# Attention scores as three products of rounded parts instead of one fp32 product, in a three-layer fp32 kernel

## What is computed

```python
# layer 1, heads of 64 channels, 8 + 8 heads, blocks of 128 queries
s = einsum('bqhd,bkhd->bhqk', qb, k) * scale + cq[..., None] - cum[..., None, :]   # forgetting heads
s = einsum('bcqhd,bckhd->bhcqk', qc, kb) * scale + bias                            # biased heads
# layer 2: 8 stick-breaking heads, 8 latent heads
z = einsum('bqhd,bkhd->bhqk', qb, k) * scale
a = exp(log_sigmoid(z) + suffix)          # suffix: reversed exclusive sum of log_sigmoid(-z)
s = (einsum(q_nope, k_nope) + einsum(q_rope, k_rope)) * scale                      # latent heads
# second block: 4 differential pairs (rotated q, k), 8 heads with three branches each
s = einsum('bqhcd,bkhcd->bhcqk', qb, k) * scale
sc, ss, sw = compressed keys, selected keys, window keys, each einsum(qb, keys) * scale
```

## Time and profile before

| | |
|---|---|
| median of three runs | 2082.27 us |
| the profiled execution | 2084.69 us |
| its span, first to last instruction | 2082.9 us |
| TensorE busy | 2029.1 us (97%), 9900 matmul records |
| VectorE busy | 993.9 us (48%), 1563 instructions |
| ScalarE busy | 904.2 us (43%) |
| GpSimd busy | 865.3 us (42%) |
| mean granted clock of TensorE | 0.995 |

### The profile page before, as it was taken

The page is one execution under the profiler, slowest core; times in us unless marked ns, Lnnn a source line. Parts: engine busy times, 40 slices in busy tenths (PEclk is TensorE's granted clock), DMA queues, the critical chain, the costliest instruction groups (busy, mean ns, idle before and its releaser), DMA issues.

```text
span 2082.9 us, 28463 instructions
## 1 busy us (share of the span) xinstructions
PE 2029.1 (97%) x9900; PEld 1596.8 (77%) x9900; DVE 993.9 (48%) x1563; ACT 904.2 (43%) x1760; POOL 865.3 (42%) x648
## 2 busy tenths in 40 slices
PE   9999999999999999999999999998989999999997
PEld 6777688888887766688888887776667878888886
DVE  6444555322264678652312265666555563223133
ACT  5444543323343664552323356765553343223234
POOL 3222345444454322244444454542114554545454
PEclk9999999999999999999999999999999999999999
DMA  4222122322222111022223232321102322232323
GB/s 157 65 70 84 58 100 93 101 92 101 91 100 91 64 58 42 31 92 100 96 97 100 91 101 71 112 92 41 42 31 71 101 91 97 95 101 92 101 94 109
DMA packets 50580, 177.87 MB, mean 85 GB/s; under 512 B 5536, under 2 KB 5800, under 8 KB 50480
## 3 DMA queue, kind: packets, MB, share of 16 engines
q1 hardware_dynamic: 48096, 172.07, 24.7%
q10 hardware_dynamic: 2384, 4.43, 0.6%
HBM read 174.36 MB, written 2.12 MB: 85 GB/s over the span
## 4 chain that ended last, share of the span: by engine, by line
issue 46%; PE 31%; POOL 19%; DVE 2%; POOLq 1%; ACT 1%; DVEq 0%; ACTq 0%
POOL w_lo L517 19%; PE gemm_banks L542 9%; PE gemm_banks L544 9%; PE gemm_banks L543 9%; PE score_banks L989 1%; PE out_bank L1035 1%; PE score_banks L998 1%; DVE turned L2217 1%; POOLq L511 0%; ACT tmp L1471 0%; POOLq L516 0%; DVE score_banks L1794 0%; DVE x L2313 0%; PE out_bank L1026 0%; PE gemm_banks L961 0%
## 5 line engine op out<-in xcount | busy, mean ns | idle before, releaser
L517 POOL TENSOR_TENSOR w_lo<-raw,w_hi 128x512 fp32r<-128x512 f32 x644 | 865.1, 1365 | 1200.4 <-ACT w_hi L1106 1200.2
L1106 ACT ACTIVATE w_hi<-raw 128x512 fp32r<-128x512 f32 x644 | 370.8, 623 | 782.5 <-PE gemm_banks L544 777.9
L542 PE MATMUL gemm_banks<-h_hi,w_hi 128*128 128x512 f32 x1512 | 612.8, 405 | 4.6 <-POOL w_lo L517 3.0
L544 PE MATMUL gemm_banks<-h_hi,w_lo 128*128 128x512 f32 x1512 | 590.5, 391 | 0.0
L543 PE MATMUL gemm_banks<-h_lo,w_hi 128*128 128x512 f32 x1512 | 589.8, 390 | 0.0
L542 PEld LDWEIGHTS gemm_banks<-h_hi,w_hi 128*128 128x128 f32 x1512 | 282.8, 187 | 98.2 <-issue 35.4
L542 PE MATMUL gemm_banks<-u_hi,w_hi 128*128 128x512 f32 x864 | 339.3, 393 | 5.6 <-POOL w_lo L517 1.5
L543 PE MATMUL gemm_banks<-u_lo,w_hi 128*128 128x512 f32 x864 | 336.3, 389 | 0.0
L544 PE MATMUL gemm_banks<-u_hi,w_lo 128*128 128x512 f32 x864 | 336.3, 389 | 0.0
L544 PEld LDWEIGHTS gemm_banks<-h_hi,w_lo 128*128 128x128 f32 x1512 | 282.8, 187 | 62.5
L543 PEld LDWEIGHTS gemm_banks<-h_lo,w_hi 128*128 128x128 f32 x1512 | 283.4, 187 | 55.7 <-issue 2.9
(11 more groups left out here) (317 smaller groups left out, 1869.0 us busy)
## 6 DMA issues: line engine op xcount, KB each, us to landing
raw<-slabs SPq DMA_DIRECT2D x322, 512.0 KB, 3.3
table<-rel_rows ACTq DMA_DIRECT2D x4, 512.0 KB, 3.5
x<-x_t SPq DMA_DIRECT2D x4, 256.0 KB, 7.0
x<-x_t ACTq DMA_DIRECT2D x4, 256.0 KB, 7.2
cos<-pos SPq DMA_DIRECT2D x2, 256.0 KB, 10.1
y_t<-x SPq DMA_DIRECT2D x2, 256.0 KB, 2.8
y_t<-x ACTq DMA_DIRECT2D x2, 256.0 KB, 2.7
y_t<-x SPq DMA_DIRECT2D x1, 512.0 KB, 2.8
```

The costliest lines, as they stand in the source:

```text
L517: pool.tensor_tensor(w_lo[:, j, part], raw[:, j, part], w_hi[:, j, part].bitcast(F32), ALU.subtract).then_inc(slab_split, 1)
L542: pe.matmul(out, high, rhs_hi, start=first, stop=False)
L544: return pe.matmul(out, low, rhs_hi, start=False, stop=last)
L1106: act.activation(w_hi[:, m % 2, part], raw[:, m % 2, part], ACT.Copy).then_inc(slab_hi, 1)
```

## The change

Each q and k that feeds a score is split by VectorE into a part rounded to fp32r and the rest (also fp32r), right behind its eviction or its rotation. A score is then three fp32r products: high times high, high times low, low times high, for both heads in turn. The columns are widened to at least 256, and so are those of the forget bias L652. The score waits for the parts (`q_parts`, `k_parts`), or for `rope_ready`, which now comes with the second part. The compressed scores take two fp32 products, with the high and with the low part of the query as they are in memory. Latent heads and all else stay. The parts lie in memory that was free or that the full tile leaves (the low part overwrites it); k_win's high part lies in `KT_hi`, k_sel's in the place of `cos1`.

```diff
                 if i == 0:
-                    pe.wait_ge(gemm_free, done["k", p])
+                    pe.wait_ge(q_parts, p + 1)
+                    pe.wait_ge(k_parts, p + 1)
...
+                n = max(w, 2 * P)
                 if p < 4:
...
-                        pe.matmul(SC[:, 2 * b + head, 0:w], fox_of[rows, p, :], fox[rows, 0:w],
+                        pe.matmul(SC[:, 2 * b + head, 0:n], fox_of[rows, p, :], fox[rows, 0:n],
                                   start=True, stop=False, skip_group_check=True)
-                for head in range(2):
-                    rows = slice(HEAD * head, HEAD * (head + 1))
-                    pe.matmul(SC[:, 2 * b + head, 0:w], q_t[rows, p % 2, i * P:w], k_t[rows, p % 2, 0:w],
-                              start=(p >= 4), stop=True, skip_group_check=True).then_inc(scored, 1)
+
+                for queries, keys in ((q_hi, k_hi), (q_hi, k_lo), (q_lo, k_hi)):
+                    for head in range(2):
+                        rows = slice(HEAD * head, HEAD * (head + 1))
+                        last = pe.matmul(SC[:, 2 * b + head, 0:n], queries[rows, p % 2, i * P:w],
+                                         keys[rows, p % 2, 0:n], start=(p >= 4 and queries is q_hi and keys is k_hi),
+                                         stop=queries is q_lo, skip_group_check=True)
+                        if queries is q_lo:
+                            last.then_inc(scored, 1)
...
-                        last = pe.matmul(bank[:, i * CQ:(i + 1) * CQ], QT[:, p % 2, i * P:(i + 1) * P], kcmp[:, :],
-                                         start=True, stop=True)
+                        pe.matmul(bank[:, i * CQ:(i + 1) * CQ], QT_hi[:, p % 2, i * P:(i + 1) * P].bitcast(F32),
+                                  kcmp[:, :], start=True, stop=False)
+                        last = pe.matmul(bank[:, i * CQ:(i + 1) * CQ], QT_lo[:, p % 2, i * P:(i + 1) * P].bitcast(F32),
+                                         kcmp[:, :], start=False, stop=True)
...
                     last.then_inc(gemm_free, 1)
                     dve.wait_ge(gemm_free, c.gemm.at())
+                    if name in "qk":
+                        qk_parts(name, p)
+
+            def qk_parts(name, p):
+
+                full = (q_t, k_t)["qk".index(name)][:, p % 2, :]
+                high = (q_hi, k_hi)["qk".index(name)][:, p % 2, :]
+                link(dve.tensor_copy(high, full))
+                dve.tensor_tensor((q_lo, k_lo)["qk".index(name)][:, p % 2, :], full, high.bitcast(F32),
+                                  ALU.subtract).then_inc((q_parts, k_parts)["qk".index(name)], 1)
...
-                    dve.tensor_tensor(dst, dst, tmp[:, 2 + n % 2, :], ALU.add).then_inc(rope_ready, 1)
+                    added = dve.tensor_tensor(dst, dst, tmp[:, 2 + n % 2, :], ALU.add)
+                    if name == "kc":
+                        added.then_inc(rope_ready, 1)
+                    else:
+                        high, low = parts_of(name, p)
+                        link(added)
+                        link(dve.tensor_copy(high, dst))
+                        dve.tensor_tensor(low, dst, high.bitcast(F32), ALU.subtract).then_inc(rope_ready, 1)
```

More of the change, by code:

```diff
@@ L366, in build @@
         w_hi, w_lo = sb("w_hi", [2, SLAB], F32R), sb("w_lo", [2, SLAB], F32R)
-        cos1, sin1, cos2, sin2 = (sb(n, [S]) for n in ("cos1", "sin1", "cos2", "sin2"))
+        region = ExitStack()
+        cos1 = sb("cos1", [S], F32, region)
+        region.close()
+        region = ExitStack()
+        k_sel_hi = sb("k_sel_hi", [S], F32R, region)
+        region.close()
+        hold = stack.enter_context(nc.sbuf_tensor("region_cos", [P, S], F32))
+        del hold
+        sin1, cos2, sin2 = (sb(n, [S]) for n in ("sin1", "cos2", "sin2"))
         consts, params = sb("consts", [N_CONST]), sb("params", [N_PARAM])
@@ L404, in build @@
         region = ExitStack()
-        k_sel, k_win = sb("k_sel", [S], F32, region), sb("k_win", [S], F32, region)
+        left = ExitStack()
+        k_sel, k_win = sb("k_sel", [S], F32, left), sb("k_win", [S], F32, left)
+        left.close()
+        k_sel_lo, k_win_lo = sb("k_sel_lo", [S], F32R, region), sb("k_win_lo", [S], F32R, region)
         V_sel, V_win = sb("V_sel", [NB, P], F32, region), sb("V_win", [NB, P], F32, region)
@@ L831, in cd_scores @@
                 if i == 0:
[L832 to L836, removed]
+                    pe.wait_ge(q_parts, 8 + p + 1)
+                    pe.wait_ge(k_parts, 8 + p + 1)
+                n = max(w, 2 * P)
+                for queries, keys in ((q_hi, k_hi), (q_hi, k_lo), (q_lo, k_hi)):
+                    for head in range(2):
+                        rows = slice(HEAD * head, HEAD * (head + 1))
+                        last = pe.matmul(SC[:, 2 * b + head, 0:n], queries[rows, p % 2, i * P:w],
+                                         keys[rows, p % 2, 0:n], start=False, stop=queries is q_lo,
+                                         skip_group_check=True)
+                        if queries is q_lo:
+                            last.then_inc(scored, 1)
             def cd_flip(s):
@@ L980, in e_scores @@
                 if br == 0:
-                    keys, need = KTT[:, p % 2, :], max(E_ROPE["q", p], E_ROPE["k", p])
+                    keys, need = (KT_hi[:, p % 2, :], KT_lo[:, p % 2, :]), max(E_ROPE["q", p], E_ROPE["k", p])
                 else:
-                    keys = (k_sel, k_win)[br - 1][:, :]
+                    keys = ((k_sel_hi[:, :], k_sel_lo[:, :]), (KT_hi[:, 0, :], k_win_lo[:, :]))[br - 1]
                     need = max(E_ROPE["nq", p], E_ROPE[("ks", "kw")[br - 1], 0])
@@ L986, in e_scores @@
                     pe.wait_ge(rope_ready, need)
-                for head in range(2):
-                    rows = slice(HEAD * head, HEAD * (head + 1))
-                    pe.matmul(SC[:, 2 * (s % 2) + head, 0:w], QT[rows, p % 2, i * P:w], keys[rows, 0:w], start=True,
-                              stop=True, skip_group_check=True).then_inc(scored, 1)
+                n = max(w, 2 * P)
+                for queries, part in ((QT_hi, 0), (QT_hi, 1), (QT_lo, 0)):
+                    for head in range(2):
+                        rows = slice(HEAD * head, HEAD * (head + 1))
+                        last = pe.matmul(SC[:, 2 * (s % 2) + head, 0:n], queries[rows, p % 2, i * P:w],
+                                         keys[part][rows, 0:n], start=(queries is QT_hi and part == 0),
+                                         stop=queries is QT_lo, skip_group_check=True)
+                        if queries is QT_lo:
+                            last.then_inc(scored, 1)
             def e_flip(s):
```

15 lines of the change are left out of this document (added).

## The result

The changed kernel takes **2133.71 us** (median of 4 runs, 2128.72 to 2136.54) against 2083.37 us before (4 runs, 2082.26 to 2084.53): a ratio of 1.0238, 95% interval 1.0226 to 1.0251. It is slower by 50.3 us, where 25.8 us (2108 us, a range up to 2117) were forecast: the sign was right, the size half of what came. The profiled execution took 2133.45 us, its span 2131.7, 48.8 more than that of before.

What follows compares the result with a forecast made beforehand. TensorE, busy for 97% of the span, was taken as the bound. Its own work -3.8, new waits +23.6 and clock +6 made +25.8 us on 2084.7, 2110.5; less 2.4 for the median, 2108 us, range 2087 to 2117 (forecast's own 2100 to 2117).

Steps and rivals of the forecast that it cites:

- Score passes: TensorE's scores: three rounded passes replace fp32 products in 24 groups of four steps, -0.30 us each, -7.2 us in all.
- A split of 3.2 us: VectorE's CAST and subtraction per tile: 3.2 us if begun behind a started GpSimd instruction, 1.2 us if not.
- no lock: Rival, chance 0.18: the CAST runs during GpSimd's first half, only the subtraction waits; split 2.0 us, kernel 2099 us.
- no collision: Rival, chance 0.12: VectorE gets ahead of GpSimd, which waits instead; every split 1.2 us, kernel 2090 us.
- six passes: Rival, chance 0.03: rounded heads don't run side by side, so six passes per step; +40 in place of -7, 2155 us.
- both other starts: First scores of stick-breaking wait for split k_t, +2.5 us; second block's start waits behind QT's and KT's splits, +3.6 us.
- stick-breaking q: Splits of q for stick-breaking pairs 1 to 3 stand uncovered ahead of the take: 3 x 3.2 = +9.6 us.
- nq: Selected and window part: three nq tile splits end ahead of shares or takes TensorE waits for, 3 x 1.2 = +3.6 us.
- absorbed waits: Rival, chance 0.10: new waits take the place of old TensorE idle time, only -3.8 us is left; 2078.5 us.
- Rest of the first mixer: Steady steps behind the first mixer's start: k's split is covered; 0.3 us added for pair 1.
- Differential part: Second block: splits of k 1 and k 2 have one to two us of cover; +1.6 us for both, bounds 0 and 4.
- Clock: TensorE gaps over 2 us may bring 3.4 us at half speed; four of seven at 1.5 us, +6, bounds 0 and 12.

Runs made afterwards that it cites:

- products_only: Changed kernel without the splits: each tile is rounded once by the instruction that writes it, and all three products read it; 2079.87 us.
- stick_later: Changed kernel with the q splits of stick-breaking pairs 1 to 3 moved from ahead of the take to behind the same step's scans; 2119.73 us.
- diff_whole: Changed kernel with pairs 1 to 3 of the differential part not split and scored by one fp32 product; 2120.30 us.
- diff_shares: Changed kernel with the differential part's splits behind the next step's maxima, take and shares, the shares moved ahead of the next rotation; 2120.10 us.
- combo: Changed kernel with q's splits behind scans, second block's behind maxima, no widening, and shares ahead of rotations in the selected and window part; 2104.23 us.
- diff_later: Changed kernel with only the differential part's splits moved, behind the next step's maxima; the second block's start left as it was; 2128.67 us.
- e_later: Changed kernel with second-block splits moved: at its start behind the next turn's eviction, in the differential part behind the next step's maxima; 2120.36 us.

## Why the prediction was right or wrong

- **Score passes, -7.2, and TensorE's own work, -3.8: right.** The step of 512 takes 0.79 for 0.81, products_only measures -3.5, the compressed scores cost 3.6 for 3.2.
- **A split of 3.2 us behind a started GpSimd, 1.2 otherwise: right.** 3.1 in the stick-breaking step, 3.2 in the differential one, 1.1 where GpSimd rested. The rivals "no lock" and "no collision" are out, and so is that of six passes.
- **First mixer's start, both other starts, stick-breaking q, nq: right.** 2.2 for 2.4; 3.0 for 2.5; 3.2 for 3.6; 8.8 for 9.6; 3.7 for 3.6. stick_later shows the mechanism: 14.0 us less with nothing changed but the place. The rival of absorbed waits is out too.
- **Rest of the first mixer, 0.3: too small.** The prediction said that above 1 us more TensorE waits for each k. In the steady pairs it doesn't, but for the last k it does (its split takes 3.2 us, from 213.01 to 216.25). There TensorE waited for the take already before the change (0.35 us at 214.16), and now it is idle for 2.47 us before the values at 218.43. I had read the steady step and not the last.
- **Differential part, 1.6 with bounds 0 and 4: wrong, 10.0.** This is the step of the waits that failed. It asked what cover the take has and left out who else is behind the split. The maxima are, and through them ScalarE's exponentials, w_hi and w_lo (5.2 of the 10.0 us); evictions (3.0) are too, and only 1.9 is the take's. What is queued behind the split was followed on VectorE and not on to ScalarE's queue and GpSimd's. diff_whole puts all ten at the splits, and diff_shares takes back 8.7 of them.
- **Clock, 4 of 7 gaps at 1.5: the size was right, the count wrong.** A single stretch cost 1.2 to 1.8 us. But six of the seven gaps of the count brought one (that at 702.33 didn't), two of them a double one, for 11.6 us in place of 6; the last k of the first mixer and two gaps of 1.8 and 1.7 us in the differential part, which had no place in the count, brought three more for 4.7 us. That makes 16.3 us. Some 1.5 us I can't place.
- **The latent heads' 1.0 us** is a wait at 907 us behind a VectorE operation that GpSimd held up in the one trace and not in the other; why the two start in another order there stayed open.

The sum missed by 23.0 us in the span: 10.1 in the waits (8.4 of them in the differential part), 12.6 in what is left over, some 11 of them the clock's, 0.3 in the passes. The range's upper end, forecast with all clock drops at 12, allowed next to nothing for a wait that had not been counted.

## What to carry to other kernels

Work that is put on an engine with half of its time free costs what the instruction behind it is late, and the one that pays may be three engines away: follow each engine's queue behind a late result until you meet the bound engine, before calling a delay covered. Where a split or a copy must be added, put it behind the last thing that anyone else waits for in the step, and not right behind an instruction that holds it up (here GpSimd's: 3.2 us for a split in place of 1.1); here that (with three pairs left whole) took back all of the 50 us. And charge a long wait of the matrix engine with more than its length: here 33.7 us of new waits came with some 17 us for slow products behind them.

## What the runs showed of the hardware

- A CAST from SBUF to rounded fp32, 128x512, takes 0.43 us. Behind a GpSimd instruction that began up to 0.15 us earlier it takes 1.40 to 1.56 us, behind one that began 0.57 us earlier 1.00 to 1.01 us: it ends some 0.3 us after GpSimd does. A subtraction of two SBUF tiles behind such a CAST takes 1.63 to 1.67 us where GpSimd has a second instruction, 0.69 alone.
- A rounded pass that follows another on half the array's rows took 0.11 to 0.12 us with 128 columns and 0.12 to 0.13 with 256: nearly the same.
- Half-clock stretches lasted 3.4 or 6.8 us (once 10.2, in combo). Each began inside a gap of TensorE or up to some 2 us behind one; the shortest such gap was 1.27 us (the one in diff_later that ends at 1455.1), and in products_only it was the 1.32 us from 873.77. But it doesn't come every time: the gap of 3.50 us in e_later that ends at 1516.3 brought none. The same gap of 2.47 us at 216 us was followed by one in the changed kernel and by none in stick_later:

```profile
218.40:221.80 3.40, 3.40 (x30) 2.66 (x31) 0.80 (x6) 2.76 (x8) 0.00 (x0) 1.00 0.04 14
```

- With that, runs of one kernel differ: of the kernel before, spans at a mean granted clock of 0.998 were 2078.2 to 2078.8 us, at 0.997 2079.6 to 2082.2, at 0.995 2082.5 to 2084.7. For a difference of 3 us, traces decide before medians do.
